# Dilated attention: the heads of a pair issued side by side, and its steps in another order

## The reference

```python
q = rms_norm(proj[:, :, gi, 0], g_q[gi]); k = rms_norm(proj[:, :, gi, 1], g_k[gi])
s = einsum('nbqhd,nbkhd->nbhqk', qb, kb) * (DIL_HEAD_DIM ** -0.5) + bias
lse = logsumexp(s); p = exp(s - lse); o = einsum('nbhqk,nbkhd->nbqhd', p, vb)
wts = softmax(stack(lses), axis=0); o = einsum('gbsh,gbshd->bshd', wts, o_all)
return o.reshape(B, S, DIL_HEADS * DIL_HEAD_DIM) @ w_o
```

## Time and profile before

| | us |
|---|---|
| median of 3 runs | 2001.74 |
| lowest, highest run | 2001.28, 2002.22 |
| span of the profiled execution | 2001.4 |
| PE busy | 1953.0 (98%) |
| DVE busy | 1418.8 (71%) |
| ACT busy | 1144.9 (57%) |

### The profile page before, as it was taken

How to read it: one execution, slowest core, us unless ns; L and a number is a source line. 1 busy time by engine, 2 the same in 40 slices (tenths; PEclk the granted TensorE clock), 3 DMA queues, 4 the chain that set the end, 5 groups by cost and what they waited for, 6 DMA issues and landing times. The chain is left out here.

```text
span 2001.4 us, 34826 instructions
## 1 busy us (share of the span) xinstructions
PE 1953.0 (98%) x14152; PEld 1812.3 (91%) x14152; DVE 1418.8 (71%) x2542; ACT 1144.9 (57%) x1941; POOL 346.9 (17%) x363
## 2 busy tenths in 40 slices
PE   8999999999999999999999999999999999999997
PEld 5799999999888889999889899999999998888886
DVE  6787776887776667657756578899987765555554
ACT  5865543556667555544755464467767754444444
POOL 0010011000000000012201010048868930000000
PEclk9999999999999999999999999999999999999999
DMA  9465687346444337656334354544444345555553
GB/s 362 158 203 197 240 282 257 119 141 238 154 146 147 119 105 236 190 187 236 136 120 159 118 189 167 183 168 159 148 158 149 139 159 188 189 189 190 189 189 116
DMA packets 97744, 356.25 MB, mean 178 GB/s; under 512 B 11105, under 2 KB 11233, under 8 KB 97201
## 3 DMA queue, kind: packets, MB, share of 16 engines
q1 hardware_dynamic: 84240, 305.04, 43.4%
q0 software_dynamic: 12624, 48.08, 7.0%
q10 hardware_dynamic: 720, 0.91, 0.1%
HBM read 352.94 MB, written 1.05 MB: 177 GB/s over the span
## 5 line engine op out<-in xcount | busy, mean ns | idle before, releaser
L2113 DVE TENSOR_TENSOR wl<-raw,wh 128x1024 fp32r<-128x1024 f32 (+1 forms) x566 | 694.2, 1230 | 393.5 <-ACT wh L1427 391.9
L1427 ACT ACTIVATE wh<-raw 128x1024 fp32r<-128x1024 f32 (+1 forms) x566 | 593.5, 1050 | 420.7 <-PE psum L598 379.4
L596 PE MATMUL psum<-peer_hh,wh 128*128 128x256 f32 x1024 | 295.6, 289 | 0.0
L598 PE MATMUL psum<-peer_hh,wl 128*128 128x256 f32 x1024 | 290.4, 284 | 0.0
L597 PE MATMUL psum<-peer_hl,wh 128*128 128x256 f32 x1024 | 290.4, 284 | 0.0
L597 PE MATMUL psum<-wl,csh 128*128 128x512 f32 x512 | 201.9, 394 | 0.0
L596 PE MATMUL psum<-wh,csh 128*128 128x512 f32 x512 | 201.8, 394 | 0.0
L598 PE MATMUL psum<-wh,csl 128*128 128x512 f32 x512 | 201.8, 394 | 0.0
L596 PEld LDWEIGHTS psum<-peer_hh,wh 128*128 128x128 f32 x1024 | 194.4, 190 | 0.0
L597 PEld LDWEIGHTS psum<-peer_hl,wh 128*128 128x128 f32 x1024 | 194.3, 190 | 0.0
L598 PEld LDWEIGHTS psum<-peer_hh,wl 128*128 128x128 f32 x1024 | 194.2, 190 | 0.0
(11 more groups left out here) (478 smaller groups left out, 4890.5 us busy)
## 6 DMA issues: line engine op xcount, KB each, us to landing
raw<-in_mlp_w SPq DMA_DIRECT2D x128, 512.0 KB, 4.2
raw<-in_eu SPq DMA_DIRECT2D x128, 512.0 KB, 3.5
raw<-in_ev SPq DMA_DIRECT2D x128, 512.0 KB, 3.4
araw<-in_ada_w POOLq DMA_DIRECT2D x76, 512.0 KB, 4.6
raw<-in_dil_qk SPq DMA_DIRECT2D x48, 512.0 KB, 3.8
raw<-in_dil_v SPq DMA_DIRECT2D x24, 512.0 KB, 3.5
raw<-in_w_in SPq DMA_DIRECT2D x16, 512.0 KB, 3.9
raw<-in_w_query SPq DMA_DIRECT2D x16, 512.0 KB, 3.5
```

What stands on the lines that cost most here:

```text
L596: e.matmul(o, l[0], r[0], start=start, stop=False, skip_group_check=loose)
L598: i = e.matmul(o, l[1], r[0], start=False, stop=stop, skip_group_check=loose)
L1427: e.activation(b.wh[v % NSPLIT][:, 0:cols], b.raw[v % NRAW][:, 0:cols], ACT.Copy).then_inc(S.hi, 1)
L2113: e.tensor_tensor(b.wl[v % NSPLIT][:, 0:cols], b.raw[v % NRAW][:, 0:cols], b.wh[v % NSPLIT][:, 0:cols].bitcast(F32), ALU.subtract).then_in ...
```

## The change

The three-stage `step` is gone. Its pieces are kinds of their own in the list: `scores`, `probs`, `turn`, `pv`, `out`, each for one `t` of a column and both heads. PE issues the two heads' scores alternately (rows 0 to 63 and 64 to 127), and the two heads' products with the values alternately (columns 0 to 63 and 64 to 127). A unit's turned probabilities go back into its own slot of `wk` (`u % 4`). DVE takes one reciprocal for both heads. Root, root square and scale move to `z` = 1, 2 and 3. Cut:

```diff
@@ dil_order
-        if c and z == 3:
+        if c and z == 1:
             out.append(("root", c - 1, 0))
-        if c and z in (3, 4):
-            out.append(("root square", c - 1, z - 3))
-        if c and z == 4:
-            out.append(("root square", c - 1, 2))
+        for g in {1: (0,), 2: (1, 2)}.get(z, ()):
+            if c:
+                out.append(("root square", c - 1, g))
...
-        if z in (0, 2, 3) or z == 5 and c < 4:
+        if z in (2, 4, 5) or z == 0 and c < 4:
             out.append(("tick", c, z))
-        if c and z in (3, 4):
-            out.append(("scale", c - 1, z - 3))
-        if c and z == 4:
-            out.append(("scale", c - 1, 2))
-        for u in {0: (4 * c - 8, 4 * c - 7), 1: (4 * c - 6, 4 * c - 5)}.get(z, ()):
-            if 0 <= u < 24:
-                out.append(("step", u, 0))
+        for g in {1: (0,), 3: (1, 2)}.get(z, ()):
+            if c:
+                out.append(("scale", c - 1, g))
+        steps = {5: [("scores", 0, 0)], 0: [("probs", 1, 0), ("scores", 1, 1)], 1: [("probs", 1, 1), ("turn", 1, 0)],
+                 2: [("turn", 1, 1), ("pv", 1, 0)], 3: [("pv", 1, 1)], 4: [("out", 1, 0)]}
+        for kind, back, t in steps[z]:
+            p = c - 1 - back
+            if 0 <= p < (7 if kind in ("scores", "probs", "turn") else 6):
+                out.append((kind, p, t))
...
-    out += [("step", 24, 0), ("step", 25, 0)]
-    tail = [(26,), (27,), (28, 29), (30, 31), (32, 33), (34,), (), ()]
+    tail = [[("pv", 6, 0), ("pv", 6, 1), ("scores", 7, 0)], [("out", 6, 0), ("probs", 7, 0), ("scores", 7, 1)],
+            [("probs", 7, 1), ("turn", 7, 0)], [("turn", 7, 1), ("pv", 7, 0)], [("pv", 7, 1)], [("out", 7, 0)], [], []]
@@ tensor_program, dilated
+        def scores(c, t):
+            tile, halves = slice(t * 128, t * 128 + 128), (4 * c + 2 * t, 4 * c + 2 * t + 1)
+            ps = [take("ds", u) for u in halves]
             pe.wait_ge(S.dve, at["dqk", "out", c, 2])
             for g in range(3):
+                for half, u in enumerate(halves):
+                    r0 = half * 64
+                    q = m.qk[r0:r0 + 64, c % 2, 2 * g, tile]
...
+                    mm(o, q, k, True, True, mark=("dil", "scores", u) if g == 2 else None)
+        def turn(c, t):
+            for u in (4 * c + 2 * t, 4 * c + 2 * t + 1):
+                ps = take("dt", u)
+                pe.wait_ge(S.dve, at["dil", "prob", u])
...
+        def pv(c, t):
...
+            for u in halves:
+                pe.wait_ge(S.act, at["dil", "probT", u])
             for kb in range(4):
+                for half, u in enumerate(halves):
+                    r = half * 64
...
+                    mm(ps[r:r + 64, t * 128:t * 128 + 128], v, wk[u % 4][:, kb * 128:kb * 128 + 128], kb == 0, kb == 3,
+                       mark=("dil", "pv", u) if kb == 3 else None)
@@ scalar_program, dilated
+        def exps(c, t):
+            for u in (4 * c + 2 * t, 4 * c + 2 * t + 1):
...
+                act(wk[u % 4], wk[u % 4], ACT.Exp, bias=m.st[:, t, 0, h:h + 1], accum_out=m.st[:, t, 1, h:h + 1],
+                    mark=("dil", "exp", u))
+        def turned(c, t):
...
+                act(wk[u % 4], bank("dt", u), ACT.Copy, mark=("dil", "probT", u))
@@ vector_program, dilated
+        def biased(c, t):
+            for u in (4 * c + 2 * t, 4 * c + 2 * t + 1):
...
+                if u >= 4:
+                    ve.wait_ge(S.pe, at["dil", "pv", u - 4])
...
+        def probs(c, t):
+            r = m.st[:, t, 1, 2 * c:2 * c + 2]
+            ve.wait_ge(S.act, at["dil", "exp", 4 * c + 2 * t + 1])
+            recip(r, r)
+            own()
+            for half in range(2):
+                u = 4 * c + 2 * t + half
+                ts(wk[u % 4], wk[u % 4], r[:, half:half + 1], None, ALU.mult, mark=("dil", "prob", u))
```

More of the change, by code:

```diff
@@ L288, in dil_order @@
         beside(8, z)
-    out += [("step", 24, 0), ("step", 25, 0)]
-    tail = [(26,), (27,), (28, 29), (30, 31), (32, 33), (34,), (), ()]
+    tail = [[("pv", 6, 0), ("pv", 6, 1), ("scores", 7, 0)], [("out", 6, 0), ("probs", 7, 0), ("scores", 7, 1)],
+            [("probs", 7, 1), ("turn", 7, 0)], [("turn", 7, 1), ("pv", 7, 0)], [("pv", 7, 1)], [("out", 7, 0)], [], []]
     for i, steps in enumerate(tail):
-        out += [("step", u, 0) for u in steps] + [("dil_w_o", i, 0)]
+        out += steps + [("dil_w_o", i, 0)]
     return out
@@ L1153, in head_sums @@
             give("headsum", c, g, sem=S.act, key=("headsum", "ms", c, g))
[L1155 to L1159, removed]
+        def scores(c, t):
+            tile, halves = slice(t * 128, t * 128 + 128), (4 * c + 2 * t, 4 * c + 2 * t + 1)
+            ps = [take("ds", u) for u in halves]
             pe.wait_ge(S.dve, at["dqk", "out", c, 2])
             for g in range(3):
[L1162 to L1178, removed]
+                for half, u in enumerate(halves):
+                    r0 = half * 64
+                    q = m.qk[r0:r0 + 64, c % 2, 2 * g, tile]
+                    k = m.qk[r0:r0 + 64, c % 2, 2 * g + 1, slice(0, 256) if g == 0 else tile]
+                    o = ps[half][:, 0:256] if g == 0 else ps[half][:, 128 + g * 128:256 + g * 128]
+                    mm(o, q, k, True, True, mark=("dil", "scores", u) if g == 2 else None)
@@ new lines, in scores @@
+            for u in halves:
+                give("ds", u, sem=S.dve, key=("dil", "biased", u))
+        def turn(c, t):
+            for u in (4 * c + 2 * t, 4 * c + 2 * t + 1):
+                ps = take("dt", u)
+                pe.wait_ge(S.dve, at["dil", "prob", u])
+                for kb in range(4):
+                    tr(ps[:, kb * 128:kb * 128 + 128], wk[u % 4][:, kb * 128:kb * 128 + 128],
+                       mark=("dil", "turned", u) if kb == 3 else None)
+                give("dt", u, sem=S.act, key=("dil", "probT", u))
@@ L1179, in s3 @@
+        def pv(c, t):
+            halves = (4 * c + 2 * t, 4 * c + 2 * t + 1)
+            if t == 0:
                 take("do", c)
             ps = b.psum[:, at["bank", "do", c], :]
-            pe.wait_ge(S.act, at["dil", "probT", u])
             pe.wait_ge(S.act, at["dv", "out", 2, c // 2])
-            r = half * 64
+            for u in halves:
+                pe.wait_ge(S.act, at["dil", "probT", u])
             for kb in range(4):
-                v = m.vt[:, c, 0, kb, r:r + 64] if kb < 2 else m.vt[:, c, kb - 1, t, r:r + 64]
-                mm(ps[r:r + 64, t * 128:t * 128 + 128], v, wk[3][:, kb * 128:kb * 128 + 128], kb == 0, kb == 3,
-                   mark=("dil", "pv", u) if kb == 3 else None)
@@ L1188, in s3 @@
-            if u % 4 == 3:
-                give("do", c, sem=S.dve, key=("dil", "out", c))
[L1191 to L1197, removed]
+                for half, u in enumerate(halves):
+                    r = half * 64
+                    v = m.vt[:, c, 0, kb, r:r + 64] if kb < 2 else m.vt[:, c, kb - 1, t, r:r + 64]
+                    mm(ps[r:r + 64, t * 128:t * 128 + 128], v, wk[u % 4][:, kb * 128:kb * 128 + 128], kb == 0, kb == 3,
+                       mark=("dil", "pv", u) if kb == 3 else None)
@@ L1199, in rows @@
+            if t:
+                give("do", c, sem=S.dve, key=("dil", "out", c))
         def rows(i):
@@ L1226, in dilated @@
                 give("dqk", i, z, sem=S.dve, key=("dqk", "out", i, z))
-            elif kind == "step":
-                step(i)
+            elif kind == "scores":
+                scores(i, z)
+            elif kind == "turn":
+                turn(i, z)
+            elif kind == "pv":
+                pv(i, z)
             elif kind == "dil_w_o":
@@ L1741, in dilated, with out_high @@
         wk = [m.work[:, i * 512:(i + 1) * 512] for i in range(4)]
[L1743 to L1757, removed]
+        def exps(c, t):
+            for u in (4 * c + 2 * t, 4 * c + 2 * t + 1):
+                h = 2 * c + u % 2
+                ac.wait_ge(S.dve, at["dil", "negmax", u])
+                act(wk[u % 4], wk[u % 4], ACT.Exp, bias=m.st[:, t, 0, h:h + 1], accum_out=m.st[:, t, 1, h:h + 1],
+                    mark=("dil", "exp", u))
+        def turned(c, t):
+            for u in (4 * c + 2 * t, 4 * c + 2 * t + 1):
+                ac.wait_ge(S.pe, at["dil", "turned", u])
+                act(wk[u % 4], bank("dt", u), ACT.Copy, mark=("dil", "probT", u))
+        def out_high(c):
+            ac.wait_ge(S.pe, at["dil", "pv", 4 * c + 3])
+            act(m.o[:, c, 0, :], bank("do", c)[:, 0:256], ACT.Copy, mark=("dil", "o hi", c))
         def compare(t, gq):
@@ L1830, in dilated @@
                 act(m.hrq[z], m.hrs[:, z, :], ACT.Square, mark=("head rs0", i, z))
-            elif kind == "step":
-                step(i)
+            elif kind == "scores":
+                exps(i, z)
+            elif kind == "turn":
+                turned(i, z)
+            elif kind == "out":
+                out_high(i)
         last_squares("dil_o", m.slots, UNIT_OF["dil_w_o", 7])
@@ L2654, in head_norm @@
```

(25 more changed lines are left out.)

## The result

The median went from 2001.29 us (10 runs) to 2005.57 us (10 runs, 2003.55 to 2008.39): ratio 1.0024, 95% interval 1.0015 to 1.0032. The change makes the kernel slower, by some 4 to 5 us; the forecast was 15. The profiled execution of the changed kernel is 2003.9 us long, 2.5 more than that of before.

A forecast was written before the change was run, and what follows sets the result against it. The prediction took PE alone to bound the kernel, busy 30.54 of 30.63 us per column. 2001.4 less 27.3 of work, plus 26.3 of waits and 16.3 of clock, gave 2016.7, forecast as 2017 us; range 1988 to 2031.

The forecast's parts named there:

- PE work after: PE's scores, values and transposes: heads' passes overlap except first and last; 7.28 against 10.69 us per column, 27.3 less over eight.
- perfect, 0.87: Lower bound for a pair's scores or values on PE: halves overlap perfectly, 0.87 us each.
- a change of shape: Loss on PE where the array's shape changes: entering costs 0.19 us for scores, 0.14 for values; leaving taken as 0.19.
- Loads that share rows: PE's value pairs: by the skill's rule they would gain nothing, some 12 us worse; the sum does not use it.
- Waits: PE's waits at head sums, transposes and the tail's bank: 30.3 us, less 4.0 there now, 26.3 more.
- The chain behind the waits: ACT and DVE queues in unit 1: head sum can start at 8.3 us, transposes at 10.8, so PE waits 1.7 and 1.65.
- The clock: After PE's longer waits the granted clock falls to 0.50 in columns 2 to 7 and the tail: 16.3 us lost.
- (a): Rival: the norms' chain on ACT is hidden and the full gain arrives, 1976 us; chance 0.15, half the waits 0.08.
- (b): Rival: PE's waits come but the clock stays at 1.00; 2001 us, 1996 with perfect overlap; chance 0.09.
- (c): Rival: the array's halves do not overlap, only 4.6 us less PE work; 2030 us; chance 0.14.

The follow-up runs named there:

- the scores together: Changed kernel with scores, bias and exponentials of t = 1 moved behind those of t = 0 in unit 5: 1976.44 us, ratio 0.9880.

## Why the prediction was wrong

The direction, the places and the mechanism were right, the size was not: 15 us slower forecast, some 4 to 5 measured. Step by step, for the stage of the profiled execution, whose 290.86 less 285.04 make 5.8 us:

- **PE work after.** This step failed most, if not by much. I let the second pass of one head run beside the first of the next, with the first and the last alone: 1.08 and 0.98 us. The passes run side by side from the first, as in the bound "perfect, 0.87". From the begin of a pair of scores to the unit behind it are 1.08 us (604.74, 605.82), against 1.27 by the terms of the forecast (1.08 + 0.10 + 0.09) and 1.07 for one head before. The stage's busy time at full clock is 262.6 - 15.8 = 246.8 us, before 280.7 - 2.8 = 277.9: **31 us less, forecast 27.3**. The costs of a change of shape fit: 0.10 + 0.87 + 0.09 is 1.06, and 1.08 was measured.
- **Loads that share rows.** Sixteen value passes in 1.09 us show that the loads of one column half run beside the other's matmuls on the same rows. By the rule of the Trainium skill (TensorE: Matmul & The Clock Gate, Part 3) the value pairs would have gained nothing; leaving it out of the sum was right.
- **Waits.** In columns 4 to 7 1.7 and 1.65 were forecast, 1.53 and 1.38 measured. In columns 2 and 3 the head sum waited 3.75 and 2.72 of 3.9 and 2.8, but the transposes only 0.43 and 0.89 of 1.65 each. There the clock fell before the end of the head sum, which took 2.04 and 1.59 us instead of 1.10; sum and wait make 2.5 us in each of columns 2 to 7. What was forecast as a wait was slow work there, so the forecast counted it twice, as a wait and as clock. Column 8 had 4.5 of 4.7, the tail 2.45 of 2.2. Together that is 26.4 of 30.3; another 2.1 came where none was forecast (1.11 at the transposes of column 1, 0.78 for a value copy, 0.21 behind the stage's last unit), so that the list adds up to 28.4.
- **The chain behind the waits.** In columns 4 to 7 the chain on ACT and DVE has the forecast's length to 0.1: from the first bias to the square 644.05 to 650.93, 6.9 us (0.80 + 0.92 + 0.71 + 1.08 + 1.29 + 1.58 + 0.52); from the scale to the transposes 651.06 to 654.13, 3.1. From the begin of unit 1 (643.28) to the head sum are 8.4 us of 8.3, to the transposes 10.85 of 10.8. So part of the difference there is only how it is counted: the profile's idle time begins at the end of the last matmul, and in a unit a matmul of 0.28 us begins every 0.12, so that the next could have begun some 0.16 earlier. The waits as a whole were off by 2 us.
- **The clock.** Forecast 16.3, from the rows 13.0. Columns 4 to 7 had falls of 3.4, 3.4, 6.8 and none; I had put the middle of the two sizes on all four. The falls' places and their two lengths were right, that one column would escape was not in the sum. Off by 3 us.
- **Sum.** 31 less, 24 of waits and 13 of clock more make 6, and the stage shows 5.8. Work, waits and clock were each off by a few us of some 30, 30 and 16, and all three the same way: together 9 us, and the difference is itself a small rest of large terms. Such a rest should have been given a lower weight than its mechanism. The range held the value.
- **Outside the stage** the changed kernel's trace is 3.3 us shorter, where nothing changed: of the falls of before, those that begin at 159.6, 733.1 and 978.8 us have none to match, and one near 361 us is new. Falls behind waits that both kernels have differ from one profiled execution to the next; it is likely that they make the spread of 5 us among the runs, but this is not shown.
- **Rivals.** (a) did not come, but its point was right: one line that puts the exponentials earlier removes the head sum's wait. That its time, 1976.4, is the price of (a), 1976, is luck: the price takes 27.3 us of work off and adds 1.8, of which it does not say how it comes about; in the stage of that trace PE is busy for 32.6 us less than before and idle for 10.0 more, and another 4.4 us are missing outside it. (b) is near what the kernel with all long waits filled does: 1997.7, its price was 1996 to 2001. (c) is out for the program's order. Where the program puts the heads in turn, the time is 2 us above the changed kernel and not the 13 by which (c) was priced above the forecast, since the waits give way and the overlap stays in part.

## What to carry to other kernels

Removing work from the engine that is the bound pays only as long as the others' queues are early enough at each hand-over. Here busy shares of 57% on ACT and 71% on DVE hid a place where ACT worked without a pause for 8 us and PE stood behind it. Walk the queues of the other engines in order, with the lengths of the trace, from the last thing that the bound engine gave them to the first that it needs back. And add the clock to the price of a wait on TensorE, as a chance and not as a rule: here 24 us of added waits brought 13 us of lost clock with them. When a gain goes missing, look first for one instruction group that can be issued earlier, before undoing the change.

## What the runs showed of the hardware that was not expected

- Products on the two halves of the rows (64*128) or of the columns (128*64) of the array run side by side completely, also in float32 where each is two passes: 12 passes in 1.15 us against 1.14 for 6, 16 in the 1.09 of 8. With the heads one after the other about two fifths of the overlap are left: 1.68 and 1.58 us against 2.0 for twice one head.
- Whether the clock falls after the same pair of waits (1.53 and 1.38 us, 1.1 apart) differs from column to column within one execution: not at all, for 3.4 or for 6.8 us. With 0.86 us of each wait filled it fell in none of these columns.
- The length of a wait does not decide it. With the heads in turn a pair of 1.66 and 1.38 us in column 3 was followed by no fall, and with the scores together a single wait of 2.50 us (before 482.90) by none. The wait of 1.51 us before 91.32 is in all ten traces: nine have the clock at 1.00 behind it, that with all long waits filled has 0.50 from 93.5 to 96.8 us. So the forecast's reading of one case each, 1.84 us with a fall and 1.51 without, was no ground for a limit between them.
- Work put into TensorE's waits made the kernel faster than the idle time did, by 10 us where all long waits were filled (by 4, at the edge of the noise, where it was in part).
